# Third attention loop of a two-block transformer kernel: ScalarE's output copies move behind the exponentials

## The chip, the cores and the metric

One core of a Trainium2 chip. The metric is the device time of one execution in microseconds (us); lower is better. Engines: TensorE (PE in the profile, PEld for its weight loads), VectorE (DVE), ScalarE (ACT), GpSimd (POOL), SyncE (SP). Each engine works through its own instructions strictly in the order in which the program lists them; semaphores tie the engines together.

## The reference

The reference runs 256 tokens of width 1024 through two transformer blocks in fp32. The part that the change touches is the attention of the last mixer (`dsa_attention`, called "odd" in the kernel): 16 heads of width 64, causal, with a selection of keys by an index score and a learned bias by distance. For one block of 128 queries it computes

```python
_, idx = lax.top_k(score, k_top)
c_sel = gather(c, idx)
s = jnp.einsum('bqhl,bqkl->bqhk', qb, c_sel) * (DSA_DH ** -0.5)
s = s + bias.transpose(0, 1, 3, 2)
s = jnp.where((dist >= 0)[:, :, None, :], s, -jnp.inf)
p = jax.nn.softmax(s, axis=-1)
return jnp.einsum('bqhk,bqkl->bqhl', p, c_sel)
```

and the result goes through two projections. Around it stand a first mixer with 16 heads, a second with 8 (called "fox") beside a gated linear attention, and six feed-forward parts.

## The kernel before

**Weights.** All weights stream through SBUF in chunks of at most 2048 columns, in the order that `plan()` writes out. SyncE loads halves of 1024 columns into `raw` (a ring of 5). For each half ScalarE copies a rounded part into `whi`, and VectorE subtracts it for the rest, `wlo`; matmuls run three passes with high and low parts. A chunk is split four chunks (`NHL`) ahead of its use. How many halves are split in each stretch of an attention loop is worked out from what TensorE has consumed there (`one_more` on ScalarE, `lows` on VectorE).

**Attention loop.** The function `attention` exists three times, once in each engine's program (line 677 for TensorE, 1387 for ScalarE, 1899 for VectorE), and is called for "first", "fox" and "odd". The odd call has 16 heads in 8 pairs; each engine runs a software pipeline over p = 0 to 9. Masks and biases are added up by GpSimd, head by head, three heads ahead, in `bias_mask` (line 2478); it starts a head when the masked-score pass of the head three before is through. In the odd call the order on each engine in step p is:

- TensorE: scores of pair p (it first waits for the masked-score passes of pair p-1, which free the two score banks, and at p = 4 and 6 for the queries q2 and q3); the weigh matmuls of pair p-2, weights `ptb` times values, which give `s_pv`; then filler steps and, between them, the two transposes (`turn_weights`) of the weights of pair p-1. The filler is the projections q2 and q3 in steps of three matmuls, and from p = 6 on the first half of the output projection (`STEPS`, `USUAL` say how many steps).
- VectorE: for both heads of pair p the masked-score pass, a custom operation that adds scores and masked bias into `xn` and takes the row extreme (line 1924), `s_smax`; then `out_lo` of pair p-2 (`ra<-pp,ra`, 128x256), which needs `s_ohs`; then the low part of a weight half; then in steps 2 and 5 `turned_` for q2 and q3 (`fa<-pp,rbb`, 128x512, line 1723 is its helper); then for both heads a reciprocal and two scalings (lines 1952, 1719) of the exponentials.
- ScalarE (lines 1399 to 1434): the output copy `out_hi` of pair p-2 (`ra<-pp`, 128x256), which waits for `s_pv` and gives `s_ohs`; four exponentials of pair p, two per head (line 1418), which wait for `s_smax` and give `s_ex`; then two copies of the turned weights of pair p-1 into `ptb` (`ptb<-pp`, 128x384), which give `s_ptc`; then the high part of a weight half.

In steps 8 and 9 there are no scores, no masked-score passes and no exponentials.

Of the kernel before, what the change touches and what calls it, by code (L numbers as in the profile page):

```python
# [163 lines left out]
def program(nc, W, XIN, XT, PT_IN, CST, GNS, GQK, GFIN, GFIN2, GLAG, FOXB, T5, OUT):  # L164
# [22 lines left out]
    with ExitStack() as ctx:  # L187
# [3 lines left out]
        def sem(name):  # L191
            return ctx.enter_context(nc.semaphore(name))

        pp = ctx.enter_context(nc.psum_tensor("pp", [128, 8, 512], F))
        ps = [pp[:, i, :] for i in range(8)]
# [36 lines left out]
        s_sc, s_smax, s_negm, s_ex, s_rcp, s_shr, s_ptn, s_ptc, s_pv, s_ohs, s_ols = [  # L232
            sem(n) for n in ("s_sc", "s_smax", "s_negm", "s_ex", "s_rcp", "s_shr", "s_ptn", "s_ptc", "s_pv",
                             "s_ohs", "s_ols")]
# [180 lines left out]
        def weights_slot(name, h):  # L415
            if name != "first":
                return pbuf[:, :, :].rearrange("p s c -> p (s c)")[:, 384 * (h % 4):384 * (h % 4) + 384]
            return pbuf[:, h % 4, :] if h % 4 < 3 else far(0, 512)

        def turn_bank(name, h):  # L420
            if name == "first":
                return 3 + h % 2
            return 3 if h % 2 and h < (4 if name == "fox" else 14) else 6

        def spans(block):
            return ((0, 256), (256, 256)) if block == "first" else (OFF, KL)

        def head_stats(hc):
            c = 16 + 6 * (hc % 8)
            return st[:, c:c + 2], st[:, c + 2:c + 4], st[:, c + 4:c + 6]  # L430
# [25 lines left out]
        def out_hi(block, j):  # L456
            return oh[:, j, :] if block == "first" else mh[:, 4 + j, :] if block == "fox" else mh[:, j, :]
# [806 lines left out]
        def scalar_program(act):  # L1264
            def copy(o, i, scale=None):
                if scale is None:
                    return act.activation(o, i, ACT.Copy, scale=1.0)  # L1267
                return act.activation(o, i, ACT.Copy, scale=scale)  # L1268
# [3 lines left out]
            def split_half():  # L1272
                j = next_half[0]
                i = halves[j][0]
                act.wait_ge(s_raw[j % NRAW], 16 * (j // NRAW + 1))
                if i >= NHL:
                    act.wait_ge(s_done, i - NHL + 1)
                copy(hi_slot(j), raw_slot(j)).then_inc(s_hi)
                next_half[0] += 1
# [107 lines left out]
            def attention(name, evict):  # L1387
                h0, pairs = HEAD0[name], COUNT[name] // 2
                off, kl = spans(name)
                causal = name != "first"  # L1390
                sbk, obk = SB[name], OB[name]
                tot = off[1] + kl[1]

                def one_more(p, at):
                    if next_half[0] < HEND[min(ended[name, p, at] - 1 + NHL, LAST)]:
                        split_half()
                    split_at[name, p, at] = next_half[0]

                for p in range(pairs + 2):
                    if p >= 2:  # L1400
                        pr = p - 2
                        act.wait_ge(s_pv, h0 + 2 * pr + 2)
                        copy(out_hi(name, pr), ps[obk[pr % len(obk)]][:, 0:256]).then_inc(s_ohs)
                    for h in (2 * p, 2 * p + 1) if p < pairs else ():
                        hc = h0 + h
                        nm, sm, rs = head_stats(hc)
                        src = stt[:, h % 2, 0:tot] if causal else ps[sbk[h % 2]][:, 0:tot]
                        if causal:
                            act.wait_ge(s_smax, 2 * (hc - 16) + 2)
                        else:  # L1410
                            act.wait_ge(s_negm, hc + 1)
                        if h >= 4:
                            act.wait_ge(s_ptn, hc - 3)
                        if h >= 8:
                            act.wait_ge(s_shr, hc - 7)
                        o = weights_slot(name, h)
                        for t in range(2):
                            y = act.activation(o[:, off[t]:off[t] + kl[t]], src[:, off[t]:off[t] + kl[t]], ACT.Exp,
                                               bias=nm[:, t:t + 1], scale=-1.0 if causal else 1.0, accum_out=sm[:, t:t + 1])
                        y.then_inc(s_ex)  # L1420
                    evict((name, p, 0))
                    if not causal or p >= pairs:
                        one_more(p, 0)
                    if 1 <= p <= pairs:
                        for par in range(2):
                            h = 2 * p - 2 + par
                            act.wait_ge(s_ptn, h0 + h + 1)
                            if h >= 2:
                                act.wait_ge(s_pv, h0 + h - 1)
                            copy(ptb[:, par, 0:tot], ps[turn_bank(name, h)][:, 0:tot]).then_inc(s_ptc)  # L1430
                            evict((name, p, 1 + par))
                    if name == "fox" and p < pairs:
                        one_more(p, 0)
                    one_more(p, 1)
# [7 lines left out]
            def first_mixer():  # L1442
# [75 lines left out]
                def evict(at):  # L1518
                    for what in beside.get(at, []):
                        tanh_gate(int(what[4:]))  # L1520

                attention("first", evict)
                after("oa0")

# [47 lines left out]
            def even_mixer():  # L1572
# [43 lines left out]
                def evict(at):  # L1616
                    for what in beside.get(at, []):
# [5 lines left out]
                        if what == "go1":  # L1623
                            out_gate(1)

                attention("fox", evict)
                evict(("fox", "end"))
                after("go1")
# [19 lines left out]
            def odd_mixer():  # L1648
# [41 lines left out]
                for c in range(2):  # L1690
                    copy(vv[:, 1, 512 * c:512 * c + 512], ps[VB[1][c]][:, :]).then_inc(s_vv)
                attention("odd", lambda at: None)
                after("oo1.0")
                proj_join("oo", 1, 8)
# [904 lines left out]
```

## Time and profile before

| | us |
|---|---|
| median of 3 runs | 1359.39 |
| lowest, highest | 1357.41, 1359.88 |
| the profiled execution | 1357.3 |
| its span in the profile | 1355.3 |
| TensorE busy | 1337.9 |
| VectorE busy | 969.8 |
| ScalarE busy | 678.7 |
| GpSimd busy | 69.6 |

The granted TensorE clock had a mean of 0.998 of full speed. Times in the rows are microseconds from the start of the span unless marked ns. The third loop lies between 1106 and 1152 us.

How to read the rows: an operation is named by engine, line, kind and out<-in; idle time in square brackets stands ahead of the operation, with what ended it. Operations overlap a little at their ends, so the spacing from one start to the next can be less than a duration. L467, L1267, L1715 and L1723 are lines of helpers that many callers share, so the operands tell the calls apart.

### The profile page before, as it was taken

What the parts mean: (1) busy time and instruction counts of PE and PEld (TensorE: products, weight loads), DVE (VectorE), ACT (ScalarE), POOL (GpSimd) and SP (SyncE); (2) the same over time, 40 slices, a digit from 0 to 9 for tenths busy, and PEclk for the clock granted to TensorE, in tenths of its full rate; (3) what the DMA queues carried; (4) which work ended last, traced back from release to release, by engine and by line L of the source; (5) the groups of instructions that cost most, each with busy time, mean ns of one, the idle gap of its engine ahead of it and who ended that gap; (6) DMA issues with size and microseconds to landing.
All of it is one profiled execution on the core that took longest, in us unless ns stands there. A gap on an engine that the chain in (4) does not pass through costs nothing.

```text
span 1355.3 us, 19411 instructions
## 1 busy us (share of the span) xinstructions
PE 1337.9 (99%) x7680; PEld 1147.4 (85%) x7680; DVE 969.8 (72%) x1326; ACT 678.7 (50%) x1057; POOL 69.6 (5%) x109
## 2 busy tenths in 40 slices
PE   9999999999999999999999999999999999999998
PEld 6988888888888888898888888888888886888886
DVE  6886677666687777657667777787776798576775
ACT  6586454444554444456554443544443567544442
POOL 0300010000000000004000000000000034000000
PEclk9999999999999999999999999999999999999999
DMA  9353556555546555464446555555554554466551
GB/s 338 114 166 115 182 176 229 186 186 188 185 141 220 198 188 186 156 204 125 147 153 218 187 187 192 178 188 196 193 192 151 182 175 130 146 204 203 186 187 47
DMA packets 67594, 241.31 MB, mean 178 GB/s; under 512 B 7999, under 2 KB 8392, under 8 KB 67504
## 3 DMA queue, kind: packets, MB, share of 16 engines
q1 hardware_dynamic: 65200, 234.19, 51.9%
q0 software_dynamic: 2016, 5.77, 1.7%
q8 instruction: 61, 1.00, 0.3%
q14 instruction: 29, 0.24, 0.1%
q10 hardware_dynamic: 288, 0.11, 0.0%
HBM read 238.88 MB, written 1.09 MB: 177 GB/s over the span
## 4 chain that ended last, share of the span: by engine, by line
PE 86%; DVE 9%; ACT 2%; issue 2%; DMA 1%; POOL 0%; SPq 0%; DVEq 0%; POOLq 0%; ACTq 0%
PE pp L467 84%; DVE wlo L1715 3%; PE pp L476 2%; DVE pbuf L1719 1%; DVE fa L1715 1%; DVE xn L1924 1%; DVE hx L1723 1%; DMA raw<-w_chunks 1%; ACT whi L1267 0%; DVE fa L1815 0%; DVE fa L2294 0%; DVE xn L1715 0%; ACT hx L1268 0%; DVE st L2290 0%; DMA fa<-f_rows 0%
## 5 line engine op out<-in xcount | busy, mean ns | idle before, releaser
L1715 DVE TENSOR_TENSOR wlo<-raw,whi 128x1024 fp32r<-128x1024 f32 (+1 forms) x444 | 522.4, 1218 | 140.3 <-ACT whi L1267 140.0
L467 PE MATMUL pp<-hx,whi 128*128 128x512 f32 (+1 forms) x2400 | 541.1, 360 | 2.1 <-DVE fa L1815 1.3
L1267 ACT ACTIVATE whi<-raw 128x1024 fp32r<-128x1024 f32 (+1 forms) x444 | 441.7, 1043 | 90.6 <-PE pp L467 81.1
L467 PEld LDWEIGHTS pp<-hx,whi 128*128 128x128 f32 x2400 | 419.7, 188 | 74.3 <-issue 8.5
L467 PE MATMUL pp<-whi,ra 128*128 128x512 f32 x1144 | 366.2, 391 | 0.0
L467 PE MATMUL pp<-hx,wlo 128*128 128x256 f32 x2032 | 314.3, 278 | 0.0
L467 PEld LDWEIGHTS pp<-hx,wlo 128*128 128x128 f32 x2032 | 278.4, 188 | 9.9
L467 PEld LDWEIGHTS pp<-whi,ra 128*128 128x128 f32 x1144 | 214.6, 188 | 43.7 <-issue 0.9
L467 PE MATMUL pp<-wlo,ra 128*128 128x512 f32 x572 | 222.7, 389 | 0.0
L1815 DVE TENSOR_REDUCE fa<-pp 128x512 f32<-128x1024 f32 x104 | 126.9, 1220 | 73.4 <-PE pp L467 73.3
L1267 ACT ACTIVATE ra<-fa 128x512 fp32r<-128x512 f32 x63 | 39.8, 632 | 227.9 <-DVE fa L1723 227.9
L1363 ACT ACTIVATE fa<-fa 128x512 f32<-128x512 f32 x44 | 27.8, 632 | 195.1 <-DVE fa L1715 195.1
L467 PEld LDWEIGHTS pp<-wlo,ra 128*128 128x128 f32 x572 | 107.4, 188 | 20.3 <-issue 0.2
L467 PE MATMUL pp<-whi,hx 128*128 128x512 f32 (+2 forms) x320 | 96.0, 376 | 1.9 <-DVE wlo L1715 1.9
L1715 DVE TENSOR_TENSOR ra<-fa,ra 128x512 fp32r<-128x512 f32 x63 | 43.6, 693 | 43.3 <-ACT ra L1267 43.3
L467 PEld LDWEIGHTS pp<-whi,hx 128*128 128x128 f32 x320 | 58.4, 188 | 17.3 <-issue 6.0
L2384 POOL TENSOR_TENSOR st<-st,cst 128x2 f32<-128x2 f32 (+3 forms) x15 | 13.4, 895 | 1162.7 <-DVE st L1720 1162.7
L467 PE MATMUL pp<-wlo,hx 128*128 128x512 f32 (+2 forms) x160 | 59.4, 371 | 0.0
L1723 DVE SCALAR_TENSOR_TENSOR fa<-fa 128x512 f32<-128x512 f32 x65 | 44.4, 683 | 2.8 <-ACT fa L1614 0.7
L1723 DVE SCALAR_TENSOR_TENSOR hx<-pp,gns,hx 128x256 fp32r<-128x256 f32 x64 | 26.5, 477 | 22.9 <-ACT hx L1268 22.9
L1306 ACT ACTIVATE xn<-X 128x512 f32<-128x512 f32 x36 | 22.4, 627 | 28.3 <-DVE X L1723 28.0
L1715 DVE TENSOR_TENSOR fa<-fa,rbb 128x512 f32<-128x512 f32 x47 | 32.4, 691 | 3.5 <-ACT fa L1603 1.1
(175 smaller groups left out, 773.0 us busy)
## 6 DMA issues: line engine op xcount, KB each, us to landing
raw<-w_chunks SPq DMA_DIRECT2D x438, 512.0 KB, 5.2
fa<-t_rows POOLq DMA_DIRECT2D x16, 128.0 KB, 3.4
fx<-x_t SPq DMA_DIRECT2D x2, 512.0 KB, 6.5
X<-x_in SPq DMA_DIRECT2D x2, 512.0 KB, 7.5
fa<-g_fin POOLq DMA_DIRECT2D x2, 512.0 KB, 4.1
fa<-f_rows POOLq DMA_DIRECT2D x8, 128.0 KB, 3.2
raw<-w_chunks SPq DMA_DIRECT2D x3, 256.0 KB, 5.7
cst<-consts POOLq DMA_DIRECT2D x1, 576.0 KB, 7.5
```

The costliest lines, as they stand in the source:

```text
L467: return pe.matmul(o, lhs, rhs, start=first, stop=last, skip_group_check=True)
L476: return pe.transpose(o, src, ident[0:n, 0:n])
L1267: return act.activation(o, i, ACT.Copy, scale=1.0)
L1306: act.activation(xn[:, t, sl], X[:, t, sl], ACT.Square, scale=1.0, accum_out=st[:, q + 2 * c + t:q + 2 * c + t + 1]).then_inc(s_sq)
L1363: act.activation(fr[:, g % 2, :], fr[:, g % 2, :], ACT.Silu, scale=1.0).then_inc(s_silu)
L1715: return dve.tensor_tensor(o, a, b, op)
L1719: return dve.tensor_scalar(o, a, s1, None, op0)
L1723: return dve.scalar_tensor_tensor(out=o, in0=a, scalar=s, in1=b, op0=op0, op1=op1)
L1815: return dve.tensor_reduce(two(o), pp[:, b:b + 2, :].rearrange("p f (s c) -> p f c s", s=2), AX.X, ALU.add)
L1924: dve.tensor_tensor_reduce(out=src[:, sl], in0=bank[:, sl], in1=more[:, sl], scale=-1.0, scalar=-GONE, op0=ALU.add, op1=ALU.min, accum_out ...
L2384: return pool.tensor_tensor(o, a, C("mhalf")[:, 0:1].to_broadcast([128, n]), ALU.pow)
```

## The change

In ScalarE's `attention` the output copy becomes a function, `out_copy`. For "first" and "fox" it is called where the code stood, ahead of the exponentials of step p. For "odd" it is called behind them, ahead of the `ptb` copies. The wait for `s_pv`, the copy itself and the count of `s_ohs` are the same, and so are the other engines' programs.

```diff
--- before.py
+++ after.py
@@ -1396,11 +1396,13 @@
                         split_half()
                     split_at[name, p, at] = next_half[0]
 
+                def out_copy(pr):
+                    act.wait_ge(s_pv, h0 + 2 * pr + 2)
+                    copy(out_hi(name, pr), ps[obk[pr % len(obk)]][:, 0:256]).then_inc(s_ohs)
+
                 for p in range(pairs + 2):
-                    if p >= 2:
-                        pr = p - 2
-                        act.wait_ge(s_pv, h0 + 2 * pr + 2)
-                        copy(out_hi(name, pr), ps[obk[pr % len(obk)]][:, 0:256]).then_inc(s_ohs)
+                    if p >= 2 and name != "odd":
+                        out_copy(p - 2)
                     for h in (2 * p, 2 * p + 1) if p < pairs else ():
                         hc = h0 + h
                         nm, sm, rs = head_stats(hc)
@@ -1418,6 +1420,8 @@
                             y = act.activation(o[:, off[t]:off[t] + kl[t]], src[:, off[t]:off[t] + kl[t]], ACT.Exp,
                                                bias=nm[:, t:t + 1], scale=-1.0 if causal else 1.0, accum_out=sm[:, t:t + 1])
                         y.then_inc(s_ex)
+                    if p >= 2 and name == "odd":
+                        out_copy(p - 2)
                     evict((name, p, 0))
                     if not causal or p >= pairs:
                         one_more(p, 0)
```

## Rows read from the trace of the kernel before

**Rows 1.** The page: busy time by engine, the chain by engine, the weight splits.

```profile
PE 1337.9 (99%) x7680; PEld 1147.4 (85%) x7680; DVE 969.8 (72%) x1326; ACT 678.7 (50%) x1057; POOL 69.6 (5%) x109
...
PE 86%; DVE 9%; ACT 2%; issue 2%; DMA 1%; POOL 0%; SPq 0%; DVEq 0%; POOLq 0%; ACTq 0%
...
L1715 DVE TENSOR_TENSOR wlo<-raw,whi 128x1024 fp32r<-128x1024 f32 (+1 forms) x444 | 522.4, 1218 | 140.3 <-ACT whi L1267 140.0
```

**Rows 2.** Waits, 1107 to 1150: waiter <- releaser, total us, times, longest us.

```profile
ACT pbuf L1418 <- DVE st L1924: 6.0, 6, 1.8
...
PE pp L467 <- ACT ptb L1267: 2.4, 4, 1.1
```

**Rows 3.** Timeline of VectorE, third loop: start, duration (us), op, [idle before <- releaser].

```profile
1116.45 0.28 DVE L1924 CUSTOM_DVE_ANT_0 xn<-pp,fa 128x128 f32<-128x128 f32 x1
...
1119.63 0.15 DVE L1952 RECIPROCAL st<-st 128x2 f32<-128x2 f32 x1
...
1122.23 0.28 DVE L1924 CUSTOM_DVE_ANT_0 xn<-pp,fa 128x128 f32<-128x128 f32 x1
...
1123.68 1.60 DVE L1715 TENSOR_TENSOR wlo<-raw,whi 128x1024 fp32r<-128x1024 f32 x1
1125.21 0.15 DVE L1952 RECIPROCAL st<-st 128x2 f32<-128x2 f32 x1
...
1127.01 0.28 DVE L1924 CUSTOM_DVE_ANT_0 xn<-pp,fa 128x128 f32<-128x128 f32 x1
...
1131.76 0.28 DVE L1924 CUSTOM_DVE_ANT_0 xn<-pp,fa 128x128 f32<-128x128 f32 x1
...
1132.87 0.42 DVE L1715 TENSOR_TENSOR ra<-pp,ra 128x256 fp32r<-128x256 f32 x1
1133.20 0.68 DVE L1723 SCALAR_TENSOR_TENSOR fa<-pp,rbb 128x512 f32<-128x512 f32 x1
...
1135.70 0.28 DVE L1924 CUSTOM_DVE_ANT_0 xn<-pp,fa 128x128 f32<-128x128 f32 x1
...
1138.65 0.15 DVE L1952 RECIPROCAL st<-st 128x2 f32<-128x2 f32 x1
...
1140.49 0.29 DVE L1924 CUSTOM_DVE_ANT_0 xn<-pp,fa 128x128 f32<-128x128 f32 x1 [0.44 <-PE pp L467]
```

**Rows 4.** Timeline of ScalarE, slots 5 and 7 of the third loop.

```profile
1131.29 0.39 ACT L1267 ACTIVATE ra<-pp 128x256 fp32r<-128x256 f32 x1 [0.99 <-PE pp L467]
1132.43 0.40 ACT L1418 ACTIVATE pbuf<-xn,st 128x128 f32<-128x128 f32 x1 [0.75 <-DVE st L1924]
...
1134.20 0.84 ACT L1267 ACTIVATE ptb<-pp 128x384 f32<-128x384 f32 x2
...
1141.33 0.39 ACT L1267 ACTIVATE ra<-pp 128x256 fp32r<-128x256 f32 x1 [0.95 <-PE pp L467]
1141.61 0.39 ACT L1418 ACTIVATE pbuf<-xn,st 128x128 f32<-128x128 f32 x1
```

**Rows 5.** Window: us, busy us of PE, PEld, DVE, ACT, POOL; granted clock; DMA.

```profile
1130.35:1135.09 4.74, 3.72 (x32) 2.76 (x32) 4.67 (x19) 3.05 (x12) 3.55 (x6) 1.00 0.59 166
1135.09:1149.42 14.33, 14.33 (x86) 10.12 (x86) 11.54 (x39) 11.18 (x29) 1.16 (x2) 1.00 0.25 78
```

**Rows 6.** Timeline of TensorE, slots 5 to 8 of the third loop.

```profile
1132.32 0.82 PE L476 MATMUL pp<-cst,pbuf 128*128 128x128 f32 x6
1133.93 0.93 PE L467 MATMUL pp<-fa 64*128 64x128 f32 x8 [0.79 <-DVE fa L1723]
1135.09 0.87 PE L467 MATMUL pp<-ptb,fa 128*64 128x256 f32 x8 [0.23 <-ACT ptb L1267]
...
1139.53 0.93 PE L467 MATMUL pp<-fa 64*128 64x128 f32 x8
...
1147.11 0.49 PE L476 MATMUL pp<-cst,pbuf 128*128 128x128 f32 x3
```

**Rows 7.** Timeline of GpSimd: a head's mask added to its bias.

```profile
1125.08 1.21 POOL L2478 TENSOR_TENSOR fa<-fa 128x128 f32<-128x128 f32 x2
```


## The prediction

> **What bounds the kernel now.** I read the page first. TensorE is busy for 99% of the span and makes 86% of the chain that ended last; VectorE makes 9% of it, ScalarE 2% [rows 1]. So a loop matters only where TensorE waits in it. The list of waits over the third loop (1107 to 1150 us) comes next: ScalarE's exponentials waited 6.0 us for the masked-score pass of VectorE, and TensorE's matmuls waited 2.4 us for `ptb`, ScalarE's copy of the turned weights [rows 2]. Nothing there says that the exponentials waited behind an output copy. The timelines show why. I call the stretch of pair p a slot, T the start of its first masked-score pass on VectorE, S the start of its score matmuls and W the start of its weigh matmuls. VectorE starts slots 2, 3, 4, 5 and 6 at 1116.45, 1122.23, 1127.01, 1131.76 and 1135.70, and has no idle time between them; the first idle time is 0.44 us ahead of slot 7 [rows 3]. TensorE's scores are ready long before VectorE comes to them. In slots 1 to 6 the loop is paced by VectorE, with TensorE catching up on filler matmuls.
>
> **What moves.** Six copies of 128x256 (pairs 0 to 5, made in slots 2 to 7) go from ahead of the four exponentials to behind them on ScalarE. Slots 8 and 9 have no exponentials, so their order stays. Nothing is added or removed and no DMA moves.
>
> **First term: what the old place costs.** An exponential starts 0.67 us after T (1131.76 to 1132.43), once the first head's pass is through. In slot 5 the copy ran at 1131.29 for 0.39 us and was over 0.75 us before the exponential could start [rows 3, 4]. The copy is hidden in slots 2 to 6. Only in slot 7 is it not: T is 1140.49, the copy ran at 1141.33, and the exponential began at 1141.61 where T alone would allow 1141.16. That is 0.45 us, in a slot whose filler covers it (TensorE is busy for all 14.33 us from 1135.09 to 1149.42 [rows 5]). Gain: 0.
>
> **Second term: the copy on the way to `ptb`.** The `ptb` copies follow 1.77 us after the first exponential (1132.43 to 1134.20) and now come one output copy later; such a copy moves its successor by 0.28 us (1141.33 to 1141.61) [rows 4]. TensorE's weigh of the next slot waits for `ptb`. This is 0.28 us in slots 2 to 5, but it runs beside the third term and is smaller.
>
> **Third term: who waits for the copy.** VectorE's `out_lo` needs the copy and stands right behind the masked-score passes, ahead of the weight splits, of `turned_` for q3 and of the reciprocals and scalings. In slot 5 it ran 1.11 us after T (1132.87) [rows 3]. Behind the exponentials the copy ends at T + 0.67 + 1.77 + 0.39 = T + 2.83 [rows 3, 4], and `out_lo` can start no sooner. VectorE stands still for 2.83 - 1.11 = 1.72 us in every slot from 2 to 7, and it is the engine without slack.
>
> How this adds up goes by the first hard deadline. TensorE's scores of slot 6 wait for q3's `turned_`, which VectorE does in slot 5 (1133.20); TensorE already stood 0.79 us for it [rows 3, 6]. The delay there is that of slots 2, 3, 4 and 5: 4 x 1.72 = 6.9 us. Against it stands relief. VectorE's reciprocals and scalings of a pair took from 1119.63 to 1122.23 = 2.60 us in slot 2 and from 1125.21 to 1127.01 = 1.80 us in slot 3 (slot 4 repeats it), but 1.40 us in slot 6 (1138.65 to 1140.49 less 0.44 idle) [rows 3]. In the long ones GpSimd was adding masks at the same time, as at 1125.08 for 1.21 us [rows 7]. GpSimd starts its masks from the same masked-score passes, so they now run while VectorE stands still and are over before the scalings. Relief: 1.2 + 0.4 + 0.4 = 2.0 us. So q3, and the scores of slot 6, come 4.9 us later, at 1138.8. The Trainium skill, SBUF — State Buffer, section "SBUF: two separate sides", calls the port pair of VectorE and GpSimd an exclusive lock in which the other engine fully blocks; the scaling that ends with the mask agrees, and without that relief the sum would be 6.9 in place of 4.9.
>
> The weigh at 1135.09 had waited another 0.3 us (0.23 on its row) for `ptb` beyond its scores; by then `ptb` will be early, and this is swallowed [rows 6]. **Sum: 6.9 - 2.0 - 0.3 = +4.6 us.** Does a later slot add to it? VectorE's q3 step starts at 1133.20 + 4.9 = 1138.1 and takes about 0.6; the scalings of slot 5 end 1.40 us behind it, at 1140.1, which is T of slot 6; its passes are through at 1141.2, and the scores of slot 7 are due at 1139.53 + 4.6 = 1144.1. A slot is then 2.83 + 0.33 (the subtraction, 1132.87 to 1133.20) + 1.22 (a split) + 1.40 = 5.8 us, so T of slot 7 is 1145.9 and head 14 is scaled 2.83 + 0.33 + 1.22 + 0.70 later, by 1151.0, while its turn is due at 1147.11 + 4.6 = 1151.7 [rows 6]. So slots 6 to 9 carry 4.6 us and add none. Behind the loop TensorE is the bound again and nothing gives it back.
>
> The profiled run took 1357.3 us (span 1355.3). The median of the runs is 1359.39, 2.1 above it, and I add the sum to that: **1364.0 us**. Bounds of the unknown relief: none at all gives 6.9 - 0.3 = +6.6. More of it, if also the weight splits of slots 3 and 4 run in 1.22 (the kernel's mean) in place of 1.60 us [rows 1, 3], gives 4.6 - 0.8 = +3.8. I take the middle value, since GpSimd's second mask of a slot still falls on the split.
>
> **Rivals.**
> - *VectorE absorbs it.* The change costs only the second term, because VectorE's late work has room before TensorE asks. For it: the weights of a pair are wanted a whole slot later. Against it: VectorE has no idle time in slots 2 to 6, and q3 was late already. Price: at most 4 x 0.28 = +1.1 us, 1360.5.
> - *Faster.* The exponentials lose their hold-up and `ptb` comes earlier, so that TensorE's waits for it shrink. Place: slots 2 to 6; price: 0.45 us, where a copy held the exponentials as in slot 7, up to the whole 2.4 us of waits [rows 2]: 1357.0 to 1358.9, not slower than before. It decides if ScalarE starts its exponentials late because of the copy. Rows 4 say that this happens once, under cover. A gain of over 2.7 us isn't in the rows.
> - *The clock falls.* The turns of slot 5 ended at 1133.14 (1132.32 + 0.82) [rows 6]. They follow the weigh of slot 5, which waits for slot 4's `ptb`: T of slot 4 is late by 2 x 1.72 - 1.6 = 1.8 us and the second term adds 0.3, so they end near 1135.2, and with the scores at 1138.8 TensorE stands 3.6 us, against 0.79 now. The granted clock was 1.00 (2.4 GHz) around the present stall [rows 5]. If it went to 1.2 GHz after the longer one, the 5.4 us of work from 1133.93 to 1139.53 would take up to twice as long: 4.6 + 5.4 = +10 us, 1369.4. No row here has a longer stall to judge by. The Trainium skill, TensorE: Matmul & The Clock Gate, section "Why this matters for your kernels", warns that idle gaps between matmul bursts bring the half clock back; this is the page's rule that speaks against the change, and no run here shows it yet.
> - That the change does nothing is out: the loop's name is "odd" in exactly this call.
>
> **Chances.** VectorE's wait as summed 0.75, absorbed 0.12, faster mechanism 0.04, clock 0.09. A measurement of this kernel can tell about 0.2%, 2.7 us, from no change. Nearly all of the first case (+3.8 and more) and the clock case lie above that; the absorbed case lies below it, and so does the low end of the faster one. So: slower 0.84, same 0.14, faster 0.02. The range takes the first case from +3.8 less, and +6.6 plus, one us or more for the runs' own spread (1357.41 to 1359.88), and some of the neighbours: 1361.0 to 1367.4.
>
> **What would show it.** Right: VectorE's `ra<-pp,ra` subtraction in the third loop idles some 1.7 us behind ScalarE's `ra` copy in six slots; masked-score passes start some 6 us apart in slots 2 to 5; TensorE waits 3 to 4 us for `fa` of L1723 ahead of slot 6; scalings shorten to about 0.55 us a head. Wrong: VectorE's idle time appears, but TensorE's wait ahead of slot 6 stays under 2 us; or the exponentials start earlier against the scores and `ptb` waits vanish; or the granted clock drops behind the stall. The rest of the kernel should only shift.

## The result, and the profile after

| | before | after |
|---|---|---|
| median, us | 1358.40 | 1365.74 |
| lowest to highest, us | 1356.94 to 1359.88 (4 runs) | 1365.35 to 1367.05 (4 runs) |
| the profiled execution, its span, us | 1357.3, 1355.3 | 1367.05, 1365.0 |
| mean granted TensorE clock | 0.998 | 0.996 |

The change makes the kernel slower: ratio 1.0058, 95% interval [1.0045, 1.0071], so about 7.9 us (6.1 to 9.6); the medians are 7.3 us apart. I had forecast +4.6.

The spans differ by 9.7 us, but not all of that is the change. The scores of slot 0, the loop's first matmuls, start at 1106.39 us before and at 1108.28 after; everything ahead of them is untouched, and over all traces of this study that point lies between 1105.78 and 1108.71. From there to the weigh matmuls of slot 9 it is 43.03 us before and 1159.10 - 1108.28 = 50.82 after: **the loop is 7.8 us longer**. I give times from the scores of slot 0 wherever traces are compared:

| us from the scores of slot 0 | before | after | later by |
|---|---|---|---|
| T of slot 2 (first masked-score pass) | 10.06 | 10.06 | 0 |
| T of slot 3 | 15.84 | 16.37 | 0.53 |
| T of slot 4 | 20.62 | 22.66 | 2.04 |
| T of slot 5 | 25.37 | 28.93 | 3.56 |
| q3 on VectorE | 26.81 | 32.11 | 5.30 |
| scores of slot 6 | 27.54 | 32.84 | 5.30 |
| scores of slot 7 | 33.14 | 40.92 | 7.78 |
| weigh of slot 9 | 43.03 | 50.82 | 7.79 |

The page of the changed kernel, to set beside [rows 1]:

```profile
span 1365.0 us, 19411 instructions
...
PE 1342.1 (98%) x7680; PEld 1149.1 (84%) x7680; DVE 967.0 (71%) x1326; ACT 677.7 (50%) x1057; POOL 68.8 (5%) x109
...
PE 85%; DVE 8%; ACT 3%; DMA 2%; issue 2%; POOL 0%; DVEq 0%; POOLq 0%; SPq 0%; ACTq 0%
```

TensorE's share is down by a point. The waits in the third loop, 1107 to 1160 us (waiter <- releaser: total, times, longest), to set beside [rows 2]:

```profile
ACT pbuf L1420 <- DVE st L1928: 14.1, 8, 3.4
DVE ra L1719 <- ACT ra L1267: 9.9, 6, 1.6
...
PE pp L467 <- ACT ptb L1267: 4.1, 4, 1.3
...
PE pp L467 <- DVE fa L1727: 3.2, 1, 3.2
```

The second line is new in six places: VectorE waits for ScalarE's output copy. The last is the stall for q3, 3.2 us where it was 0.8. VectorE's timeline shows one after the other, as in [rows 3]:

```profile
1118.34 0.28 DVE L1928 CUSTOM_DVE_ANT_0 xn<-pp,fa 128x128 f32<-128x128 f32 x1
...
1121.17 0.42 DVE L1719 TENSOR_TENSOR ra<-pp,ra 128x256 fp32r<-128x256 f32 x1 [1.65 <-ACT ra L1267]
...
1124.65 0.28 DVE L1928 CUSTOM_DVE_ANT_0 xn<-pp,fa 128x128 f32<-128x128 f32 x1
...
1127.48 0.43 DVE L1719 TENSOR_TENSOR ra<-pp,ra 128x256 fp32r<-128x256 f32 x1 [1.64 <-ACT ra L1267]
1127.83 1.88 DVE L1719 TENSOR_TENSOR wlo<-raw,whi 128x1024 fp32r<-128x1024 f32 x1
1129.63 0.15 DVE L1956 RECIPROCAL st<-st 128x2 f32<-128x2 f32 x1
...
1130.94 0.29 DVE L1928 CUSTOM_DVE_ANT_0 xn<-pp,fa 128x128 f32<-128x128 f32 x1
...
1137.21 0.28 DVE L1928 CUSTOM_DVE_ANT_0 xn<-pp,fa 128x128 f32<-128x128 f32 x1
...
1140.05 0.42 DVE L1719 TENSOR_TENSOR ra<-pp,ra 128x256 fp32r<-128x256 f32 x1 [1.64 <-ACT ra L1267]
1140.39 0.68 DVE L1727 SCALAR_TENSOR_TENSOR fa<-pp,rbb 128x512 f32<-128x512 f32 x1
...
1142.81 0.29 DVE L1928 CUSTOM_DVE_ANT_0 xn<-pp,fa 128x128 f32<-128x128 f32 x1 [0.42 <-PE pp L467]
```

Each `ra` subtraction has 1.64 or 1.65 us of idle time ahead of it (9.9 us for six in the waits). In slot 5 it starts 1140.05 - 1137.21 = 2.84 us after T, where it was 1.11. ScalarE's timeline of slot 5 has the new order, to set beside [rows 4]:

```profile
1137.89 0.40 ACT L1420 ACTIVATE pbuf<-xn,st 128x128 f32<-128x128 f32 x1 [3.40 <-DVE st L1928]
...
1139.66 0.36 ACT L1267 ACTIVATE ra<-pp 128x256 fp32r<-128x256 f32 x1
1139.92 0.84 ACT L1267 ACTIVATE ptb<-pp 128x384 f32<-128x384 f32 x2
```

The exponentials start 0.68 us after T, as before (0.67); the copy follows 1.77 us later and `ptb` 0.26 us behind it. The exponentials gained nothing. GpSimd's masks in slot 3, as in [rows 7]:

```profile
1125.45 1.14 POOL L2482 TENSOR_TENSOR fa<-fa 128x128 f32<-128x128 f32 x2 [0.85 <-DVE st L1928]
...
1127.47 1.15 POOL L2482 TENSOR_TENSOR fa<-fa 128x128 f32<-128x128 f32 x2
```

The first mask now lies in VectorE's idle time, but the second (1127.47 to 1128.62) lies on the weight split at 1127.83, which took 1.88 us; the scalings behind it are short. Before, the same mask lay beside the split at 1123.68, which took 1.60 us [rows 3]:

```profile
1123.03 1.16 POOL L2478 TENSOR_TENSOR fa<-fa 128x128 f32<-128x128 f32 x2
```

That mask had 0.51 us to go when the split started; now it has 0.79 us to go. The split grows by the difference, 0.28 us. TensorE around the stall, to set beside [rows 6]:

```profile
1136.70 1.20 PE L476 MATMUL pp<-cst,pbuf 128*128 128x128 f32 x6
1141.12 1.66 PE L467 MATMUL pp<-fa 64*128 64x128 f32 x8 [3.22 <-DVE fa L1727]
1142.71 1.55 PE L467 MATMUL pp<-ptb,fa 128*64 128x256 f32 x8
```

The turns of slot 5 end at 1137.90, the scores of slot 6 start at 1141.12: 3.22 us. The scores then take 1.66 us in place of 0.93, and the weigh 1.55 in place of 0.87. The windows say why, where [rows 5] had 1.00 (the clock is the third column from the end):

```profile
1136.00:1138.00 2.00, 1.77 (x12) 1.08 (x10) 1.93 (x13) 0.11 (x1) 0.00 (x0) 1.00 0.70 131
1138.00:1140.00 2.00, 0.00 (x0) 0.00 (x0) 0.41 (x4) 2.00 (x10) 1.99 (x4) 1.00 0.55 209
1140.00:1141.00 1.00, 0.00 (x0) 0.00 (x0) 0.95 (x3) 1.00 (x4) 0.23 (x1) 0.69 0.00 0
1141.00:1147.00 6.00, 5.88 (x23) 3.83 (x24) 3.86 (x17) 2.84 (x10) 1.14 (x2) 0.50 0.00 0
1147.00:1148.00 1.00, 1.00 (x7) 0.91 (x6) 0.93 (x6) 0.42 (x1) 0.00 (x0) 0.90 0.00 0
1148.00:1156.00 8.00, 8.00 (x53) 5.55 (x51) 4.53 (x18) 5.88 (x17) 0.00 (x0) 1.00 0.24 76
```

TensorE did nothing from about 1138 on; the granted clock fell from 1.00 between 1140 and 1141, was 0.50 (1.2 GHz) until 1147 and back at 1.00 (2.4 GHz) from 1148 on.

### The profile page after: what moved, and what is told of

Read it like the earlier page. It is cut to its first block, busy times and chain, and to the rows that moved or that the text cites. A ratio compares the mean times of both kernels' runs of the same rounds, so it can differ in the third digit from the quotient of the medians.

```text
span 1365.0 us, 19411 instructions
## 1 busy us (share of the span) xinstructions
PE 1342.1 (98%) x7680; PEld 1149.1 (84%) x7680; DVE 967.0 (71%) x1326; ACT 677.7 (50%) x1057; POOL 68.8 (5%) x109
## 4 chain that ended last, share of the span: by engine, by line
PE 85%; DVE 8%; ACT 3%; DMA 2%; issue 2%; POOL 0%; DVEq 0%; POOLq 0%; SPq 0%; ACTq 0%
PE pp L467 83%; DVE wlo L1719 3%; DMA raw<-w_chunks 2%; PE pp L476 2%; ACT whi L1267 1%; DVE pbuf L1723 1%; DVE hx L1727 1%; DVE xn L1928 1%; ACT pbuf L1420 0%; DVE fa L1819 0%; DVE fa L1719 0%; ACT hx L1268 0%; ACT fa L1267 0%; DVE fa L2298 0%; ACT fa L1268 0%
```

## The experiments

My theory (A): VectorE is the engine without slack in slots 2 to 5, its queue stands still behind the masked-score passes for the late copy, q3 carries that to TensorE, and the clock falls behind the stall as a second, separate cost. The main rival (B): the cost is ScalarE's own order, through `ptb`. The other letters stand for smaller rivals and are explained in the expectations. The edits are against the changed kernel unless it says otherwise; `...` stands for lines left out. All costs are against the kernel before on the same chip, with the 95% interval of the ratio. "In the trace" is the weigh of slot 9 against 43.03 us; it comes from the one run of each kernel that was profiled, and where that run is not typical of the others I say so.

**1. `out_lo` behind the weight split.**

```diff
+                def low_part(pr):
+                    dve.wait_ge(s_ohs, h0 // 2 + pr + 1)
+                    tt(out_lo(name, pr), ps[obk[pr % len(obk)]][:, 0:256], out_hi(name, pr).bitcast(F),
+                       ALU.subtract).then_inc(s_ols)
...
-                    if p >= 2:
-                        pr = p - 2
...
+                    held = name == "odd" and 2 <= p < pairs
+                    if p >= 2 and not held:
+                        low_part(p - 2)
...
                     lows(p - 1, 1)
                     if not states:
                         evict((name, p, 0))
+                    if held:
+                        low_part(p - 2)
```

> The changed kernel, but in steps 2 to 7 of the third loop VectorE does its subtraction out_lo behind the weight split and the q2/q3 step, ahead of the reciprocals; ScalarE keeps the new order. Theory A (the cost is VectorE standing still behind the masked-score passes for a copy that now comes at T + 2.83): work of 1.2 to 1.8 us now fills that time, VectorE idles under 0.5 us for the copy in slots 2 to 4, TensorE waits under 1.2 us ahead of slot 6, the clock stays at 1.00, and the time is that of the kernel before, 0 to +1 us. Rival B (the cost is on ScalarE: the ptb copies, and with them TensorE's weigh matmuls, come later): out_lo's place changes nothing, +5 us or more stay.

Measured: 1360.51 against 1358.03, ratio 1.0021 [1.0013, 1.0030]; in the trace 46.35, +3.3. Most of the cost is gone, which B can't give, but not all of it, and less than A said. VectorE's timeline of slot 3, and GpSimd's mask beside it:

```profile
1124.61 1.25 DVE L1719 TENSOR_TENSOR wlo<-raw,whi 128x1024 fp32r<-128x1024 f32 x1
1126.34 0.42 DVE L1719 TENSOR_TENSOR ra<-pp,ra 128x256 fp32r<-128x256 f32 x1 [0.47 <-ACT ra L1267]
1126.68 0.15 DVE L1961 RECIPROCAL st<-st 128x2 f32<-128x2 f32 x1
1126.87 1.77 DVE L1723 TENSOR_SCALAR pbuf<-pbuf,st 128x128 f32<-128x128 f32 x2
...
1128.75 0.55 DVE L1723 TENSOR_SCALAR pbuf<-pbuf,st 128x128 f32<-128x128 f32 x2
```

```profile
1127.33 1.15 POOL L2487 TENSOR_TENSOR fa<-fa 128x128 f32<-128x128 f32 x2
```

The idle time is down to 0.47 us here, 0.50 in slot 4 and 1.04 in slot 5. But now the scaling meets the mask that had met the split: the two scalings of the first head took 1.77 us, those of the second 0.55. What VectorE wins by the place of `out_lo` it partly loses to GpSimd. T of slots 3, 4, 5 comes at 15.49, 21.20 and 26.88, 1.5 us late at the last. The clock fell here too, behind waits of 1.14 and 0.82 us (experiment 7). The profiled run is the slowest of the 11, and its mean clock of 0.996 is that of three of them only; the others have 0.998 or 0.999. The 3.3 us of the trace are thus an upper end, and the medians are 2.5 us apart.

**2. The wait alone, in the kernel before.**

```diff
+                        if name == "odd" and p < pairs:
+                            dve.wait_ge(s_ex, h0 + 2 * p + 2)
                         dve.wait_ge(s_ohs, h0 // 2 + pr + 1)
```

> The kernel before with its old order on ScalarE; only VectorE's out_lo in steps 2 to 7 also waits for the four exponentials of the step. Theory A: VectorE stands still about 1.4 us in each slot (the exponentials end near T + 2.5), slots 2 to 5 add 5.6 us less some 1.6 us of masks that now run in the idle time, +4 us, and about 2.7 more if TensorE's stall ahead of slot 6 is long enough for the clock to fall: +4 to +7. Rival B (ScalarE's order costs): within 1 us of the kernel before.

Measured: 1364.01 against 1358.03, ratio 1.0049 [1.0035, 1.0062]; in the trace 50.29, +7.3. ScalarE's order is the old one and the cost is nearly all there. VectorE idles 1.37 to 1.38 us in slots 2 to 5 here (1.64 in the changed kernel), T of slot 5 comes at 29.03 (28.93 there), and the scores of slot 6 at 32.67 after a stall of 2.96. B is out. The wait is 0.27 us shorter, but the split behind it grows by the same amount: 2.15 us in slot 3 in place of 1.88, beside a mask of GpSimd that starts 0.09 us ahead of it and so has 1.06 us to go, where it had 0.79. Slot 3 is 6.29 us long on VectorE in both.

**3. Work without use in the stall.**

```diff
                     if p == 6:
+                        for _ in range(14):
+                            mm(ps[2][:, :], hh[:, 0, 0:128], flat(hx[:, 1, :, :]), True, True)
                         pe.wait_ge(s_qT, 4)
```

> The changed kernel with 14 matmuls of 128x512 without use (into a free bank) ahead of TensorE's wait for q3 in step 6, some 3.2 us of work in the stall. Theory A with the clock as a second, separate cost: the granted clock stays at 1.00 behind the stall, slot 6 takes 5.4 to 5.6 us again and not 8.1, and the cost against the kernel before falls from 7.5 to about 5 us. Rival C (slot 6 is slow for another reason, such as late weights or copies): slot 6 stays near 8 us and the time does not fall.

Measured: 1363.88 against 1358.03, ratio 1.0042 [1.0029, 1.0055]; in the trace 48.06, +5.0. Windows of this run, split at the scores of slots 6 (1138.65) and 7 (1143.94):

```profile
1134.00:1138.65 4.65, 4.46 (x23) 3.15 (x21) 2.97 (x15) 3.24 (x12) 2.24 (x4) 1.00 0.46 137
1138.65:1143.94 5.29, 5.29 (x34) 3.75 (x34) 3.57 (x16) 3.68 (x13) 1.15 (x2) 1.00 0.00 0
1143.94:1154.00 10.06, 10.06 (x63) 7.06 (x64) 8.04 (x26) 7.11 (x17) 0.00 (x0) 1.00 0.37 113
```

The scores of slot 6 come at 32.87, where the changed kernel has 32.84: the useless matmuls cost nothing. The clock stays at 1.00, slot 6 takes 5.29 us and not 8.08, and 2.8 us of the loop are back. Rival C, a slot 6 that is slow for another reason, is out. So in the traces the 7.8 us are 5.0 of waiting and 2.8 of half clock. The whole runs say the same less sharply: the profiled run is the fastest of the five (1361.73, the others 1363.76 to 1364.07), and by the ratios the cost falls from 7.9 to 5.7 us, 2.2 us less, with intervals that overlap.

**4. The new order in steps 2 to 4 alone.**

```diff
-                    if p >= 2 and name != "odd":
+                    if p >= 2 and not (name == "odd" and p < 5):
                         out_copy(p - 2)
...
-                    if p >= 2 and name == "odd":
+                    if p >= 2 and name == "odd" and p < 5:
                         out_copy(p - 2)
```

> The changed kernel with the new order in steps 2, 3 and 4 alone. Theory A: three waits of 1.72 us, less 1.6 of relief and 0.3 at the weigh of slot 6: +3.3 us; TensorE's stall ahead of slot 6 is 1.5 to 2.5 us and the clock stays at 1.00, so the clock's 2.7 us are gone at once with one wait. Rival D (each moved copy costs the same, 7.5 / 6 = 1.25 us): +3.8 us with the clock falling as before, only later.

Measured: 1363.09 against 1358.03, ratio 1.0038 [1.0025, 1.0050]; in the trace 48.00, +5.0. The scores of slot 6 come at 31.25, 3.7 us late (I said 3.6: the 3.3 and the 0.3 that the weigh swallows). But behind a stall of only 1.50 us the clock fell to 0.50 for about three microseconds, which I had not expected; that is the rest. Both forecasts of the time, +3.3 and rival D's +3.8, were too low.

**5. q3 ahead of `out_lo` in step 5.**

```diff
+                    first = (name, p) == ("odd", 5)
+                    if first:
+                        evict((name, p, 0))
                     if p >= 2:
                         pr = p - 2
                         dve.wait_ge(s_ohs, h0 // 2 + pr + 1)
...
-                    if not states:
+                    if not states and not first:
                         evict((name, p, 0))
```

> The changed kernel, but in step 5 VectorE does the q3 step ahead of its subtraction out_lo and so ahead of that step's wait for the copy. Theory A (q3 is the deadline through which VectorE's waits reach TensorE): q3 and the scores of slot 6 come 1.72 + 0.34 = 2.1 us earlier than in the changed kernel, 3.3 us later than before in place of 5.3; the clock still falls behind the shorter stall as in the run with steps 2 to 4, for some 1 to 1.5 us; +4 to +5 us in all. Rival E (TensorE's bound in these slots is ptb, and q3 only seems to be waited for): the weigh of slot 6 takes its time over from q3 and +7 stays.

Measured: 1362.50 against 1358.25, ratio 1.0033 [1.0020, 1.0045]; in the trace 47.25, +4.2. The scores of slot 6 come at 30.80, 3.3 us late as expected, so q3 is the deadline. In the profiled run the clock stayed at 1.00 around the stall, where I had expected it to fall. `ptb` was the next thing late, as the second wait of TensorE's timeline shows:

```profile
1139.51 0.93 PE L467 MATMUL pp<-fa 64*128 64x128 f32 x8 [1.16 <-DVE fa L1727]
1141.26 0.87 PE L467 MATMUL pp<-ptb,fa 128*64 128x256 f32 x8 [0.82 <-ACT ptb L1267]
```

The weigh of slot 6 starts 3.60 us after T of slot 5 here (32.55 - 28.95) and 3.33 after it before (28.70 - 25.37): the second term of the prediction, 0.27 us, counts in full as soon as q3 is out of the way.

**6. The new order in steps 6 and 7 alone** (`p > 5` in the edit of 4).

> The changed kernel with the new order in steps 6 and 7 alone. Theory A: VectorE's two waits of 1.7 us fall behind the q3 deadline and under TensorE's filler: 0, within 0.7 us of the kernel before, clock at 1.00. Rival D (each moved copy costs the same): 2 of 6 parts of 7.5, +2.5 us.

Measured: 1358.19 against 1358.25, ratio 1.0000 [0.9992, 1.0009]; in the trace 43.15, +0.1. VectorE idles 1.65 and 1.64 us for the copies in these two slots, and nothing waits for it. Copies that cost alike (D) are out: what a wait costs depends on the slot.

**7. Experiment 1 with 6 matmuls without use in its stall.**

> The run with out_lo behind the weight split, with 6 matmuls of 128x512 without use (1.4 us) ahead of the wait for q3 in step 6, to fill its 1.1 us stall. If the rest of its cost there was half clock again, slot 6 takes 5.4 us in place of 6.9 and the cost against the kernel before falls from 2.8 us to about 1.3. If not, it stays at 2.8 or grows by the matmuls' excess of 0.3.

Measured: 1359.82 against 1358.25, ratio 1.0015 [1.0006, 1.0024]; in the trace 44.81, +1.8, and 1.5 us less than in experiment 1. From the weigh of slot 6 to that of slot 7 it is 5.29 us in place of 6.85: in that trace the clock had taken 1.6 us behind two short waits. By the medians the cost falls by 0.9 us only, from 2.5 to 1.6, with intervals that overlap; the profiled run of experiment 1 was its slowest.

**8. The new order in step 5 alone** (`p == 5`).

> The changed kernel with the new order in step 5 alone, the step whose VectorE queue holds the q3 step. Theory A: one wait of 1.72 us straight on the deadline: the scores of slot 6 come 1.7 us later than before (29.3 us from the scores of slot 0), the weigh of slot 6 some 1.5, and the loop ends 1.4 to 1.7 us later, or 2.5 to 3 if the clock falls behind a stall of 2.5 us. Rival D (each moved copy costs the same): one of 6 parts of 7.5, +1.2 us, with the clock at 1.00.

Measured: 1360.63 against 1359.04, ratio 1.0017 [1.0009, 1.0026]; in the trace 45.80, +2.8. The scores of slot 6 come at 29.06, 1.5 us late, behind a stall of 2.52 us. Between the medians it is 1.6 us. Its windows:

```profile
1136.00:1138.00 2.00, 0.51 (x6) 0.51 (x8) 1.55 (x5) 2.00 (x6) 0.60 (x1) 1.00 0.04 14
1138.00:1140.00 2.00, 2.00 (x13) 0.81 (x11) 1.82 (x12) 0.08 (x1) 0.55 (x2) 0.54 0.00 0
1140.00:1142.00 2.00, 2.00 (x8) 1.62 (x7) 1.47 (x3) 1.89 (x8) 0.59 (x1) 0.61 0.00 0
1142.00:1144.00 2.00, 2.00 (x13) 1.65 (x12) 1.33 (x7) 0.99 (x4) 0.00 (x0) 1.00 0.28 92
```

The clock fell for some 3 us in the profiled run. It probably did not in all; only one is traced, but of the 12 runs 5 took 1362.03 to 1363.15 us, all at a mean granted clock of 0.996, and 7 took 1359.67 to 1360.76 at 0.997 or 0.998.

**9. A try for a better kernel,** against the kernel before: its order on ScalarE, q3 first as in 5, and VectorE's splits of steps 3, 4 and 5 in steps 6, 7 and 8.

```diff
                 def lows(p, at):
+                    if name == "odd" and 2 <= p < 7:
+                        p = {2: 1, 3: 1, 4: 1, 5: 2, 6: 3}[p]
                     while next_half[0] < split_at.get((name, p, at), 0):
```

> A try for a better kernel: the old order on ScalarE; VectorE does the q3 step of step 5 ahead of out_lo, and the weight splits that it had in steps 3, 4 and 5 move to steps 6, 7 and 8, where it has idle time. Theory A (VectorE paces slots 2 to 6 in the kernel before): slots 3 and 4 shrink by 1.2 to 1.6 us on VectorE, TensorE's waits of 3.2 us in the loop fall to 1 or less, 1 to 2.5 us faster than before. Rival F (TensorE's own work or ptb paces the loop): within 0.5 us of the kernel before.

Measured: 1357.23 against 1358.25, ratio 0.9993 [0.9985, 1.0002]; in the trace 41.99, -1.0. The loop is 1 us shorter, but VectorE won only 0.5 us a slot (T of slot 4 at 20.10, of slot 5 at 24.32) where I had expected 1.2 to 1.6. Without the split, the scalings stand beside the masks: those of slot 3 took 0.55 + 1.58 us in place of 1.04 + 0.55, and VectorE also waits for the exponentials now, 0.16 us ahead of the first reciprocal. A gain of this size can't be told from no change.

**10. The new order with the splits of 9.**

> The changed kernel with its new order on ScalarE, and on VectorE the weight splits of steps 3, 4 and 5 moved to steps 6, 7 and 8 and the q3 step ahead of out_lo in step 5. Theory A (the new order costs only because VectorE has no slack for a wait of 1.7 us): the wait stays at 1.6 to 1.7 us in each slot, but takes the place of a split of 1.2 to 1.8; slots 3 and 4 are 4.6 to 5.0 us long on VectorE as before, the scores of slot 6 come within 0.7 us of before, the clock stays at 1.00, and the time is within 1 us of the kernel before in place of 7.5 above it. Rival B (ScalarE's order itself costs): 3 us or more stay.

Measured: 1360.04 against 1359.04, ratio 1.0006 [0.9997, 1.0014]; in the trace 44.55, +1.5. VectorE's timeline of slots 4 and 5:

```profile
1124.10 0.28 DVE L1930 CUSTOM_DVE_ANT_0 xn<-pp,fa 128x128 f32<-128x128 f32 x1
...
1126.93 0.43 DVE L1719 TENSOR_TENSOR ra<-pp,ra 128x256 fp32r<-128x256 f32 x1 [1.64 <-ACT ra L1267]
1127.27 0.16 DVE L1961 RECIPROCAL st<-st 128x2 f32<-128x2 f32 x1
...
1128.99 0.28 DVE L1930 CUSTOM_DVE_ANT_0 xn<-pp,fa 128x128 f32<-128x128 f32 x1
...
1131.82 0.43 DVE L1719 TENSOR_TENSOR ra<-pp,ra 128x256 fp32r<-128x256 f32 x1 [1.64 <-ACT ra L1267]
```

The wait of 1.64 us is there in full, yet slot 4 is 4.89 us long (4.75 before), since nothing but the scalings stands behind it. The clock stayed at 1.00. Against the kernel before, the time can't be told from no change, as A said.

But the kernel before is not the like of this one. Experiment 9 is: it differs in ScalarE's order alone. There slots 3 and 4 are 4.26 and 4.22 us long in place of 4.89, the scores of slot 6 come at 26.68 in place of 28.08, and the loop ends at 41.99 in place of 44.55. So with q3 first and a split's time more room on VectorE in slots 3 to 5, the same change costs 2.6 us in the traces (ratios 1.0006 and 0.9993, about 1.8 us, with intervals that just overlap), where it cost 7.8. VectorE's missing slack is most of the cost, not all of it. The rest also comes through `ptb`: the weigh of slot 6 waits for it.

```profile
1137.48 0.87 PE L467 MATMUL pp<-ptb,fa 128*64 128x256 f32 x8 [0.83 <-ACT ptb L1267]
```

It starts 2.18 us later than in experiment 9, of which 1.91 are T of slot 5 and 0.27 the second term; another wait of 0.33 us for `ptb` follows at slot 8, where experiment 9 has none.

## Why the prediction was right, and what was mis-sized

**What bounds the loop: right.** VectorE's queue paces slots 2 to 5; delays put on it reach TensorE (2), and the same delays in slots 6 and 7 don't (6).

**First term, nothing gained: right.** The exponentials start 0.68 us after T in slot 5 as before. In slot 7 they no longer wait for the copy, and no engine profits.

**Second term, 0.28 us through `ptb`: right in size** (0.26 from the copy to the next). Experiments 1 and 2 show that it is not the main cost. In the changed kernel it moves the weigh of slots 4 and 5 (3.61 and 3.60 us after the T before them, where it was 3.34 and 3.34) and is hidden at slot 6 behind the later q3; where q3 is early (experiments 5 and 10) it counts.

**Third term, 1.72 us a slot: right.** `out_lo` ran 2.84 us after T where I had 2.83; the idle time in the trace is 1.64, since a start overlaps the end ahead of it by 0.08.

**Relief of 2.0 us: too large.** T moves by 0.53, 1.51, 1.52 and q3 by another 1.74 us; less than 4 x 1.72 = 6.9 by 1.6 in all. By slot that is 1.2 in slot 2, as I had it, but 0.2 in slots 3 and 4 in place of 0.4. I had let GpSimd's masks end ahead of the scalings, and they do, but the second one then lies on the split, which grew from 1.60 to 1.88 us. I had named that collision as a reason not to count on a shorter split, and not that it could make the split longer. Scores of slot 6: +5.3 measured, +4.9 forecast. The 0.3 us at the weigh of slot 6 were swallowed as forecast: 5.3 - 0.3 = 5.0, and experiment 3 gives 5.0.

**The clock: the term that I left to a rival.** I had worked out that TensorE would stand for 3.6 us (3.2 measured) and gave the fall of the clock a chance of 0.09 at +5.4 us. It fell, in the trace, and cost 2.8 us there (experiment 3), half of my price, which had let all of slot 6 take twice as long. The warning of the Trainium skill, TensorE: Matmul & The Clock Gate, section "Why this matters for your kernels", came true: the clock was at 0.50 behind the gap of 3.22 us and stayed at 1.00 where the gap was filled. The case that happened is thus the first one and the clock rival together, which my list of cases held apart. So the sum should have been 4.6 + 2.8 = 7.4, and the time stayed inside the range (1361.0 to 1367.4) because that had room for part of it. The sign and the mechanism of the delay held. Of my signs of being right all four came (six waits of 1.64 or 1.65 us, passes 6.3 us apart, 3.22 us for q3, scalings of 0.55 to 0.65), and so did one of being wrong, the granted clock dropping behind the stall.

**Luck in the number.** 1364.0 lies 1.7 us below the measured 1365.74, but the sum was short by 2.7 (4.6 against 7.3 between the medians). The base hid 1.0 of that: I had stood on 1359.39, the median of three runs, and with the fourth run it is 1358.40.

**"Absorbed"** and **"faster"** are out by experiments 2 and 4 and by the unchanged start of the exponentials.

## What to carry to other kernels

Before moving an instruction on an engine with slack, look at who waits for it on an engine without slack, and at what stands behind that wait: here a copy of 0.36 us, moved by 1.7 us, held up the whole queue of VectorE, though its own result was wanted much later. The cost runs to the first hard deadline (q3) and is nothing behind it. If the sum shows TensorE standing still for microseconds, price the half clock behind it in the same sum, and test it by filling the stall with matmuls without use.

## What was not expected

- The clock fell behind shorter waits than the changed kernel's 3.22 us: 2.52 us (experiment 8), 1.50 us (experiment 4) and 1.14 + 0.82 us (experiment 1), and stayed at 1.00 behind 1.16 + 0.82 us (experiment 5) in the runs that were profiled. In experiment 8 the times of the same program fall into two groups, some 2 us apart, which I take for both outcomes. The length of a single wait doesn't decide it here; what does was not tried.
- Where a GpSimd mask of 1.15 us lies, a VectorE operation between SBUF tensors grows: the scalings before (2.60 us for a pair of heads), the split after (1.88), a scaling of one head in experiment 1 (1.77). The Trainium skill, SBUF — State Buffer, section "SBUF: two separate sides", describes this as an exclusive lock, and these rows agree. For the split they even give the size: it takes 1.22 us alone, and beside a mask with 0.51, 0.79 or 1.06 us to go it took 0.38, 0.66 or 0.93 us more (slot 3 before, changed, and in experiment 2), each time what was left of the mask less 0.13. In experiment 1 a mask was the one to grow, to 2.14 us, beside a split of 1.25. This moved the cost about, and spoiled the gain of experiments 1 and 9.
